# Sums of the modulation slices in quarters, each behind a quarter of a projection

## The reference, cut to what matters

```
mod = silu(c) @ ada_w[i] + ada_b[i]          # 1024 x 6144 matrix, one row out
sh1, sc1, g1, sh2, sc2, g2 = split(mod, 6)
h   = norm(x) * (1 + sc1) + sh1              # shift and scale before a mixer
x   = x + g1 * norm(mixer(h))                # gate behind it
h   = norm(x) * (1 + sc2) + sh2 ; x = x + g2 * norm(feed_forward(h))
```

## Time and profile before

| | |
|---|---|
| median of 3 runs | 2141.95 us (2141.62 to 2142.88) |
| profiled execution, its own time | 2144.28 us |
| its span, first to last instruction | 2142.5 us |
| mean granted TensorE clock | 0.959 of full |
| feed-forward input, about | 205 to 333 us |
| feed-forward output, about | 333 to 401 us |
| first mixer of block two, about | 406 to 690 us |
| expert layers and pooling mixer | the rest |

### The profile page before, as it was taken

One profiled execution on the slowest core, in us unless ns is written; L12 is line 12 of the kernel. 1 busy time (PEld: TensorE's weight loads), 2 busy tenths in 40 slices (PEclk: granted clock), 3 DMA queues, 4 the chain that ended last, 5 costly groups with the idle time before them and its releaser, 6 DMA issues.

```text
span 2142.5 us, 21985 instructions
## 1 busy us (share of the span) xinstructions
PE 1797.3 (84%) x7101; PEld 1069.2 (50%) x7101; DVE 1465.7 (68%) x3029; ACT 906.1 (42%) x2357; POOL 603.7 (28%) x567
## 2 busy tenths in 40 slices
PE   4888999899988889997788877898898877787776
PEld 3757998788876544442232222355444422222322
DVE  6676957767776767766667767526777677667675
ACT  2446423434473344444444444313444444444442
POOL 1160000000000343543344343103444434343441
PEclk7889989999999999999999999999999999999999
DMA  9753748555655799999999999566999999999995
GB/s 369 273 197 121 282 177 313 194 200 211 236 197 187 313 421 422 420 421 418 420 421 422 422 421 422 243 255 248 421 422 421 421 421 421 421 421 422 421 422 236
DMA packets 114690, 723.76 MB, mean 338 GB/s; under 512 B 11504, under 2 KB 13344, under 8 KB 34064
## 3 DMA queue, kind: packets, MB, share of 16 engines
q0 software_dynamic: 74864, 540.30, 60.8%
q1 hardware_dynamic: 39712, 182.07, 23.2%
HBM read 721.24 MB, written 1.08 MB: 337 GB/s over the span
## 4 chain that ended last, share of the span: by engine, by line
DMA 43%; PE 26%; DVE 17%; ACT 7%; issue 5%; POOL 2%; SPq 0%; DVEq 0%; ACTq 0%; POOLq 0%
DMA X<-in_k_uv,EI 24%; DMA Z<-in_k_uv,EI 11%; PE PS L2141 7%; DMA W<-in_k_uv,EI 5%; DVE junk L1821 4%; PE PS L1834 3%; PE PS L1836 3%; PE PS L1835 3%; DVE WL L1457 3%; DVE ACC L1441 3%; PE PS L2118 2%; DMA W<-in_ada_w 2%; PE PS L1927 2%; POOL X L1002 1%; ACT WH L1011 1%
## 5 line engine op out<-in xcount | busy, mean ns | idle before, releaser
L2141 PE MATMUL PS<-X,dg 128*128 128x512 f32 x1344 | 651.4, 617 | 143.8 <-ACT dg L1011 142.9
L1821 DVE CUSTOM_DVE_ANT_0 junk<-H,X 128x1024 f32<-128x1024 f32 x336 | 410.8, 1223 | 255.6 <-DMA X<-in_k_uv,EI 243.4
L2141 PEld LDWEIGHTS PS<-X,dg 128*128 128x128 f32 x1344 | 240.3, 193 | 521.8 <-ACT dg L1011 324.3
L1002 POOL DMA_INDIRECT X<-in_k_uv,EI x336 | 361.4, 1076 | 458.4 <-PE PS L2141 285.0
L1011 ACT ACTIVATE CF<-DOT 128x1 f32<-128x1 f32 x512 | 103.7, 203 | 681.8 <-DVE DOT L1821 679.8
L2141 PE MATMUL PS<-Z,dg 128*128 128x512 f32 x520 | 256.2, 622 | 59.9 <-ACT dg L1011 59.4
L1821 DVE CUSTOM_DVE_ANT_0 junk<-H,Z 128x1024 f32<-128x1024 f32 x130 | 158.9, 1222 | 94.6 <-DMA Z<-in_k_uv,EI 87.3
L1002 POOL DMA_INDIRECT Z<-in_k_uv,EI x130 | 137.6, 1058 | 303.4 <-PE PS L2141 165.3
L1011 ACT ACTIVATE dg<-CP,CG 128x128 f32<-128x128 f32 x512 | 205.5, 401 | 16.8
L2141 PEld LDWEIGHTS PS<-Z,dg 128*128 128x128 f32 x520 | 92.9, 193 | 202.1 <-ACT dg L1011 127.9
L1834 PE MATMUL PS<-XH,WH 128*128 128x256 f32 x592 | 174.6, 295 | 4.2 <-DVE WL L1457 2.2
(11 more groups left out here) (316 smaller groups left out, 2608.8 us busy)
## 6 DMA issues: line engine op xcount, KB each, us to landing
W<-in_ada_w SPq DMA_DIRECT2D x56, 1024.0 KB, 5.3
Y<-in_ada_w SPq DMA_DIRECT2D x16, 1024.0 KB, 5.9
W<-in_k_win SPq DMA_DIRECT2D x16, 1024.0 KB, 5.0
W<-in_k_ffi SPq DMA_DIRECT2D x13, 1024.0 KB, 6.0
Y<-in_k_ffi SPq DMA_DIRECT2D x9, 1024.0 KB, 4.9
W<-in_ffn_w_out SPq DMA_DIRECT2D x8, 1024.0 KB, 6.1
W<-in_peer_wq SPq DMA_DIRECT2D x8, 1024.0 KB, 22.2
X<-in_peer_wq SPq DMA_DIRECT2D x7, 1024.0 KB, 13.0
```

The lines of the kernel that those rows point to most:

```text
L1002: e.indirect_dma_start(out=WS[k][:, :], out_offset=None, in_=I[f"k_uv{ly}"][:, :], in_offset=bass.IndirectOffsetOnAxis(ap=EI[t][:, j:j + 1 ...
L1821: e.tensor_tensor_reduce(junk, H[:, t, :], d[:, 0:D], 1.0, 0.0, ALU.mult, ALU.add, DOT[:, j:j + 1]).then_inc(v_dot, 1)
L2141: p = e.matmul(PS[:, 2 * t + q, :], dgb[n % 4][:, :], d[:, D + q * 512:D + (q + 1) * 512], start=(j == 0), stop=(j == 127))
```

## The change

In the feed-forward layers, the two slices that stood ahead of part 26 are now spread over parts 26 and 27, and the slice ahead of part 39 over part 39: behind each quarter of the projection come four of the slice's sixteen matmuls, and `mod` follows the last. In the mixer, a complete slice goes into `due` as four parts. The next call of `step` marks the bank (`ripe`) and issues nothing else; from then on `sums()`, called at every k ahead of the projection's quarter, issues one part each. Calls of `step` that fall while parts are due issue nothing. `places` now has k == 0 of every n from 0 to 13.

By the list that follows from this, in the mixer (n, k):

| step | before | after |
|---|---|---|
| ada 47 | (0,4) | (0,0) |
| sum of slice 6 | (1,4) | (0,4) (1,0) (1,1) (1,2) |
| ada 48 to 55 | (1,4) to (5,0) | the same |
| sum of slice 7 | (6,0) | (5,4) (6,0) (6,1) (6,2) |
| ada 56 to 63 | (6,0) to (9,4) | (6,4) to (10,0) |
| sum of slice 8 | (10,4) | (10,4) (11,0) (11,1) (11,2) |
| ada 64, 65, 66 | (10,4) (11,0) (11,4) | (11,4) (12,0) (12,4) |
| ada 67, 68, 69 | (12,4) (13,0) (13,4) | (13,0) (13,4) (15,4) |
| ada 70, 71 | (15,4) (16,4) | (16,4) (17,4) |

```diff
+    def gemm_mod(n, s, *banks):
+
+        for q in range(4):
+            P("gq", n, q, *banks)
+            P("modp", s, 3, q)
+        P("mod", s, 3)
...
-        if i == 16:
-            mod(3, 3)
-            mod(4, 3)
-        gemm(n, bank(low))
+        if i in (16, 17):
+            gemm_mod(n, i - 13, bank(low))
+        else:
+            gemm(n, bank(low))
...
         if i == 7:
-            mod(5, 3)
-        gemm(n)
+            gemm_mod(n, 5)
+        else:
+            gemm(n)
...
-    due = []
+    due, ripe = [], []
 
     def step(b):
 
-        if len(due) > 1:
-            mod(due[0], b)
-            due.clear()
-        elif due:
-            due.append(None)
+        if due:
+            ripe.append(b)
             return
         m = next(steps, None)
         if m is not None:
             ada(m)
             if m in mods:
-                due.append(mods[m])
+                due.extend((mods[m], part) for part in range(4))
+
+    def sums():
+
+        if due and ripe:
+            s, part = due.pop(0)
+            P("modp", s, ripe[0], part)
+            if part == 3:
+                P("mod", s, ripe[0])
+                ripe.clear()
...
-    places = (1, 2, 3, 4, 5, 6, 7, 8, 9, 10, 11, 13)
+    places = range(14)
...
                 elif kind == "modp":
-                    s, b = a
+                    s, b = a[:2]
+                    lo, hi = (4 * a[2], 4 * a[2] + 4) if len(a) > 2 else (0, 16)
...
-                    take(b)
-                    for j in range(16):
+                    if lo == 0:
+                        take(b)
+                    for j in range(lo, hi):
...
-                    p.then_inc(p_mod, 1)
-                    free[b] = [(v_mod, s + 1)]
+                    if hi == 16:
+                        p.then_inc(p_mod, 1)
+                        free[b] = [(v_mod, s + 1)]
```

More of the change, by code:

```diff
@@ L284, in make_plan @@
             step(5)
+        sums()
         next(g)
```

## The result

The changed kernel takes 2132.05 us (median of 5 runs, 2130.52 to 2135.19), the kernel before 2142.88 beside it (5 runs, 2141.62 to 2149.48): ratio 0.994, 95% interval 0.9927 to 0.9953. A second series on another chip gave 2133.09 (2130.95 to 2133.39) against 2145.19, ratio 0.994 again (0.9927 to 0.9953). The forecast was faster, at 2132.9. Its time fits better than its difference: -9.1 of 2141.95 is a ratio of 0.9958, just outside the interval; by the medians -10.8 and -12.1 us were measured, against the kernel before beside each. The profiled execution took 2130.52 us for its span of 2128.7.

The account below looks back on a forecast made before the run. Expert layers run at DMA's pace, the first block at PE's, with half clock around the one-column sums and DVE pacing parts of the mixer. Gains and costs summed to -9.1 us from 2141.95, giving 2132.9; 8-in-10 range 2127.5 to 2139.5.

Parts of the forecast that it names:

- The clock stays up: PE at the spread sums: quarters of 0.9 us between projection quarters keep granted clock 1.00; the one large assumption.
- The slower rival: Parts 26 and 27: the mix holds the clock at half throughout, 11.5 us lost, 2153 from this place alone; chance 0.05.
- Slices 3 and 4, -7.3: Feed-forward input: the bank wait of 1.46 us goes and 12.00 us at half clock take 6.0; 7.3 us gained.
- Slice 5, -1.7: Feed-forward output: the 3.50 us at about half clock behind the sum go; 1.7 us gained.
- Switches, +1.2: PE: each extra block costs about 0.08 us, three extra for each of six slices; 1.2 us lost, between 0 and 1.4.
- Slice 6, -1.7: Mixer: 3.50 us at half clock go, 1.7 us gained, with `ada 47` at (0,0) just in time.
- Slice 7 and (6,4), -2.65: Mixer: 1.65 us of clock at slice 7, and 1.0 from a shorter DVE addition at (6,4).
- Slice 8, +1.25: Mixer: additions on DVE at (10,0) and (12,0) delay `dm(12)`, so a loss of 1.25 us instead of a 1.7 gain.
- End of the mixer, +1.8: `ada 71` at (17,4) delays the transposed head behind `hs2(3)`; 1.8 us lost, ends 0 and +2.35.
- the rival with all of DVE's moves covered: DVE's moved additions cost nothing: -13.85 us, 2128.1; chance 0.14.
- One sign that I had named: End of the mixer: line 1651 (the fold) about 9 us earlier than before instead of 11.

Follow-up runs that it names:

- e2: The kernel before with only the mixer part of the change, feed-forward layer as before: 2144.09 us against 2145.30, ratio 0.9993.
- e5: The changed kernel with one more addition ahead of the double loop, so all later ones come one place earlier: 2135.97 us against 2145.19 for the kernel before.
- e12: The changed kernel with slice 8 in two halves at (10,4) and (11,0): 2135.98 us against 2144.65 for the kernel before, ratio 0.9953.
- e3: The kernel before with slices 3 and 4 whole, one ahead of part 26, the other ahead of part 27: 2139.19 us against 2145.30, ratio 0.9974.
- e7: The changed kernel with DVE's additions at their old places, slice 7 in halves: 2153.23 us against 2145.19 for the kernel before, ratio 1.0038.
- changed, again: The changed kernel unchanged, run and profiled again on another chip: 2133.09 us against 2145.19 for the kernel before, ratio 0.994.
- e10_order_whole: The changed kernel with each mixer sum whole at the place of its last quarter, DVE's order kept: 2143.61 us against 2144.65 for the kernel before.
- e11: The changed kernel with slice 8 whole at its old place, no addition at (12,0): 2134.06 us against 2144.65 for the kernel before, ratio 0.9942.
- e1: The kernel before with only the feed-forward layer changed, mixer as before: 2137.49 us against 2145.30, ratio 0.9965.
- e4: As e1, but the feed-forward sums in halves of 1.84 us: 2136.68 us against 2145.30 for the kernel before, ratio 0.996.
- e9: As e4, but three quarters of each feed-forward sum in the first piece, the last in the second: one run, 2138.98 us against 2144.65 before.

## Why the prediction was right, point by point

**The clock stays up: right, with a condition.** 34 times in the profiled executions a quartered sum began without a wait of PE directly ahead of it (three in the feed-forward layer of nine executions, slice 6 in seven), and the clock fell at none. 12 times it began behind a wait of 1.1 to 1.2 us (slices 7 and 8), and the clock fell at 4 (both in e2, slice 8 in e5, slice 7 in e12). I named that place as the weak one and gave it no price; that both profiles of the changed kernel kept the clock there is luck in part. The slower rival, in which the mix holds the clock down, never came near: 24.00 us at 1.00. The row on thin matmuls (M under 512) in the Trainium skill, "TensorE: Matmul & The Clock Gate", section "Why this matters for your kernels", has the clock swing at every K-tile unless all K-tiles run ahead of the next DMA. That is a case of waits for DMA, and no run here shows it: 22 of the 28 whole sums lost the clock with no wait of PE directly ahead of them.

**Slices 3 and 4, -7.3: measured -7.21** or -7.22 in nine executions of eight kernels. Here the sum by steps was nearly exact. e3 splits it: 2.6 without the long wait, in an execution with three stretches of half clock left, the rest the clock.

**Slice 5, -1.7:** -1.75 and -1.55.

**Switches, +1.2: wrong, they cost nothing.** This is the largest term that failed. A part with its sum takes four periods of 2.32 us, 9.3; before, it was 3.49 for the block and 5.76 + 0.08 for the part, also 9.3. I had taken the 0.08 by which a projection's quarter is longer behind a sum, and not seen that four short blocks take less than the long one: each of them gives way to the next projection matmul after 0.81 (285.07 to 285.88), 3.24 for the four instead of 3.49.

**Slice 6, -1.7:** -2.23 and -1.56. `ada 47` at (0,0) came just in time, as worked out: no wait ahead of the first quarter. e7, which leaves it at (0,4), shows what that place costs: a wait of 6.03 us.

**Slice 7 and (6,4), -2.65: measured -3.25, and both terms are there.** The wait of 1.2 is there (1.20). Counted from `dm(2)`, the maxima of these units come later (+) or earlier than in the kernel before:

| kernel | `dm(6)` | `dm(7)` | `dm(9)` | clock at slice 7 |
|---|---|---|---|---|
| changed | -2.21 | -3.26 | -3.25 | kept |
| changed, again | -2.23 | -3.29 | -3.28 | kept |
| e2_mixer_only | -0.57 | -1.62 | -1.61 | down from 510.8, ahead of `dm(6)` |
| e12_eight_halves | -0.66 | -1.72 | -1.70 | down from 502.9, ahead of `dm(6)` |
| e10_order_whole | -4.89 | -4.84 | -3.39 | down from 516.7, `dm(6)` at 516.82 |

From `dm(6)` to `dm(7)` the first four rows gain 1.05: that is DVE's shorter pair, forecast at 1.0. At `dm(6)` the rows that kept the clock are 1.6 ahead of those that lost it: that is the clock, forecast at 1.65. DVE was not the pace at `dm(6)`; ACT waited there for PE, and DVE for ACT, in the kernel before:

```profile
524.55 0.60 ACT L1011 ACTIVATE K<-PS 128x512 f32<-128x512 f32 x1 [5.88 <-PE PS L1836]
...
526.13 2.36 DVE L1457 TENSOR_TENSOR WL<-W,WH 128x1024 fp32r<-128x1024 f32 x2 [3.54 <-ACT WH L1011]
...
528.41 1.21 DVE L1606 TENSOR_REDUCE st<-PS 128x2 f32<-128x1024 f32 x1
```

The 0.6 that is left had no term in the forecast. The last quarter of the sum, at 512.23, begins behind what ACT waits for here (511.99) and so no longer stands ahead of `dm(6)`; by the sum's length that is worth up to 0.87, an estimate.

**Slice 8, +1.25:** +1.49 in both executions. `dm(10)` 2.27 later for 2.35, `dm(12)` behind its new addition. e11, which makes the trade the other way, comes out the same.

**End of the mixer, +1.8: measured +1.28 and +1.81, but the cause is not shown.** The addition stands where I put it, and the head behind it comes 2.88 us after `hs2(3)` instead of 1.23, so 1.65 late. But at 655.00 PE also ran at half clock, and e11, without that addition and with its head 1.22 behind `hs2(3)`, is as late at the fold (+1.77):

```profile
650.31 0.69 DVE L1663 TENSOR_TENSOR OB<-OB,st 128x512 f32<-128x512 f32 x1
651.53 0.54 DVE L1506 TENSOR_SCALAR XT<-PS,gn,zero 128x256 f32<-128x256 f32 x1 [0.53 <-PE PS L1973]
...
666.26 1.23 DVE L1672 TENSOR_TENSOR H<-R,R 128x1024 f32<-128x1024 f32 x1 [4.84 <-DMA R<-in_ln_b]
```

```profile
651.50:655.00 3.50, 3.50 (x11) 0.52 0.00 0
```

Behind the 2.2 us that PE waits for `hs2(3)` the clock fell in 8 of the 14 profiled executions, in four with the addition and four without; there the stretch was +0.84 to +2.01, in the other six 0 to +0.81. All four executions with the addition had the fall. Among the eight with the fall, the four with the addition have +1.72 on average and the four without it +1.48, with a scatter of more than the difference. So what the addition costs by itself stays open, between 0 and 1.3; whether it makes the fall more likely stays open too.

**The sum.** The terms give -9.1; the steps of the profile up to the fold give -11.7 without the entry. The difference of 2.6 is 1.2 of switches, 0.6 at slice 7, 0.5 each at slice 6 and at the end, less 0.2 at slice 8. The total of -13.8 in that execution, which is the number of the rival with all of DVE's moves covered, is a coincidence: `dm(10)` and `dm(12)` show them uncovered, and 3.0 of it lie behind the fold. One sign that I had named came out the other way: the fold (line 1651, here 1667) was to be about 9 us earlier and not 11, and it was 10.9 earlier (680.10 to 669.25) and in the second profile 10.1, because the terms fell short. That the time lands within 1 us of 2132.9 is luck in part: by the medians the gain is 1.7 larger than forecast, and the kernel before took 0.9 more beside the changed one than the median that I started from.

**What the forecast lacked.** It took the parts as independent. Timed, the layer alone gives 0.9965 and the mixer alone 0.9993, which multiplied make 0.9958, and both together 0.994. The profiles point to two reasons. In the mixer alone slices 7 and 8 lost the clock behind their waits (1.6 and 1.5 us). And behind the changed layer the whole sums of the mixer lost more clock (6.8 + 3.5 + 3.4 us in e1, 3.5 + 7 + 7 in e4) than in the kernel before (3.5 + 3.3 + 3.4), so there is more for the quarters to save. These are single executions, and the intervals nearly allow the product; the reasons are likely, not shown.

## What to carry to other kernels

Thin matmuls that have to be done somewhere on a busy TensorE should be spread in short pieces (here 0.95 us) between wide ones, with TensorE not waiting ahead of a piece: here two parts and their sums took 7.2 us less, a wait of 1.5 included. Move the producer first, since a piece that stands in TensorE's queue ahead of its input costs the wait, the clock, and more than the whole sum did. Price a lost clock from the place it falls in: 1.6 us where TensorE sets the pace, 8.9 where a stall and a thin block meet (slice 8 of e10). And look at more than one execution before you call a clock kept: the same place kept it in one and lost it in another.

## What the runs showed of the hardware

- One-column work with no wait directly ahead: pieces of 0.95 to 1.05 us between projection quarters kept 1.00 at 34 sums of 34, pieces of 1.84 us at 3 of 3 (e4); 2.74 us lost it at 3 of 3 (e9, one execution). With blocks of 3.63 us, waits ahead or not, the clock is at 0.50 at 26 sums of 28; at three of these it was down before the block began.
- An idle of 1.07 or 1.20 us and then a half sum of one-column work (1.84 us elsewhere) lost the clock, 2 times of 2 (e12, e7); an idle of 1.1 to 1.2 and then 1.05 lost it 4 times of 12, in kernels with the same instructions around it. Each stretch of 3.4 us at 0.50 cost 1.5 to 1.7 us where PE set the pace; that this makes much of the scatter of a kernel's runs is likely, and not shown.
- The same place in the work can keep or lose the clock without any sum near it: behind the wait of 2.27 us that PE has at the end of the feed-forward input, the clock fell in 12 of the 14 profiled executions (334.1 to 337.5 before) and not in e3 and e4, which wait there as long.
- The clock can stay at 0.50 through 17.00 us of busy PE, when a stall, a few matmuls and a block of one-column ones follow each other (e10).
